# Key selection with three bits per two chunks and a third block on ScalarE; differential attention with its first odd scores in banks 4 to 7

## The reference

```
def diff_attention(q, k, v, lam, rel_bias):      # 4 heads, 8 query blocks of 128
    sc = einsum('cbhqd,cbhkd->cbhqk', qblk, kt) + bias      # c = 0, 1
    p = softmax(sc, axis=-1)
    a = p[0] - lam * p[1]
    return einsum('bhqk,bhkv->bhqv', a, vt)

def sparse_attention(q, k, v, q_idx, k_idx, w_idx):
    ...
    score = einsum('bth,bths->bts', wb, relu(logits))
    score = where(causal, score, -inf)
    _, idx = top_k(score, 256)
    ...                      # softmax attention over the 256 keys of each query
```

## Time and profile before

| what | us |
| --- | --- |
| median of 3 runs | 3103.51 |
| lowest and highest | 3095.89, 3104.91 |
| the profiled execution | 3112.71 |
| its span | 3110.2 |
| TensorE busy | 2694.9 |
| VectorE busy | 2020.7 |
| ScalarE busy | 1566.0 |
| GpSimd busy | 1153.8 |

### The profile page before, as it was taken

How to read it: one execution, slowest core, us unless ns; L and a number is a source line. 1 busy time by engine, 2 the same in 40 slices (tenths; PEclk the granted TensorE clock), 3 DMA queues, 4 the chain that set the end, 5 groups by cost and what they waited for, 6 DMA issues and landing times. The chain is left out here.

```text
span 3110.2 us, 41522 instructions
## 1 busy us (share of the span) xinstructions
PE 2694.9 (87%) x14032; PEld 2113.8 (68%) x14032; DVE 2020.7 (65%) x4318; ACT 1566.0 (50%) x3035; POOL 1153.8 (37%) x981
## 2 busy tenths in 40 slices
PE   6999788898979997988989796997889696997887
PEld 5877565676868775656777585775667584775666
DVE  4472377798434724877984348897767348897766
ACT  3221276798322113767872216675764316675761
POOL 0100166665001002765640002983741002983731
PEclk9999898999989997999999899998999899998899
DMA  4443210100324421101013110110031101110022
GB/s 123 119 139 102 85 40 8 41 1 33 117 70 124 143 82 37 39 8 41 1 56 128 51 24 24 48 45 24 1 120 71 61 21 28 48 41 25 1 88 81
DMA packets 90750, 181.93 MB, mean 58 GB/s; under 512 B 12552, under 2 KB 27912, under 8 KB 90504
## 3 DMA queue, kind: packets, MB, share of 16 engines
q1 hardware_dynamic: 74124, 150.69, 15.4%
q10 hardware_dynamic: 16416, 28.61, 3.2%
HBM read 149.87 MB, written 33.33 MB: 59 GB/s over the span
## 5 line engine op out<-in xcount | busy, mean ns | idle before, releaser
L1355 POOL TENSOR_SCALAR a_prob<-a_prob,a_ratio 128x1024 f32<-128x1024 f32 x64 | 71.9, 1123 | 536.7 <-DVE a_ratio L1314 536.7
L718 PE MATMUL ps<-w_hi,hh 128*128 128x512 f32 (+1 forms) x640 | 242.7, 379 | 22.2 <-DVE w_lo L603 10.1
L718 PE MATMUL ps<-w_lo,hh 128*128 128x512 f32 (+1 forms) x640 | 241.0, 377 | 0.0
L718 PE MATMUL ps<-w_hi,hl 128*128 128x512 f32 (+1 forms) x640 | 239.3, 374 | 0.0
L1792 PE MATMUL ps<-o_w_hi,hh 128*128 128x512 f32 x512 | 212.1, 414 | 24.3 <-DVE o_w_lo L1716 24.3
L2253 DVE TENSOR_SCALAR_CACHE_REDUCE select_rows<-masks,select_cuts 128x1024 bf16<-128x1024 int16 (+7 forms) x264 | 231.2, 879 | 0.2
L1792 PE MATMUL ps<-o_w_hi,hl 128*128 128x512 f32 x512 | 207.6, 406 | 0.0
L1792 PE MATMUL ps<-o_w_lo,hh 128*128 128x512 f32 x512 | 206.7, 404 | 0.0
L1303 DVE CUSTOM_DVE_ANT_0 a_prob<-ps,a_bias 128x1024 f32<-128x1024 f32 x128 | 151.6, 1222 | 83.2 <-PE ps L1443 83.2
L1772 POOL TENSOR_TENSOR o_rstd<-o_rstd,nhalf 128x1 f32<-128x1 f32 x56 | 46.6, 833 | 411.9 <-DVE o_rstd L1653 238.7
L1034 POOL TENSOR_SCALAR b_prob<-b_prob,a_guest_small 128x1024 f32<-128x1024 f32 x128 | 144.2, 1127 | 129.4 <-DVE a_guest_small L978 126.8
(11 more groups left out here) (356 smaller groups left out, 7942.5 us busy)
## 6 DMA issues: line engine op xcount, KB each, us to landing
w_early<-in_w_in SPq DMA_DIRECT2D x108, 256.0 KB, 2.8
ada_w<-in_w_ada ACTq DMA_DIRECT2D x96, 256.0 KB, 2.8
w_raw<-in_w_in SPq DMA_DIRECT2D x84, 256.0 KB, 2.8
ak<-gates SPq DMA_DIRECT2D x32, 256.0 KB, 3.8
xcur<-aq SPq DMA_DIRECT2D x16, 512.0 KB, 3.8
y<-xcur SPq DMA_DIRECT2D x16, 512.0 KB, 3.7
a_bias<-bias_tiles SPq DMA_DIRECT2D x8, 960.0 KB, 5.2
bq<-in_w_out SPq DMA_DIRECT2D x12, 512.0 KB, 4.1
```

The source lines that it names most:

```text
L718: mm = nc.tensor.matmul(o, lhs, rhs, start=(k == 0 and i == 0), stop=(k == K - 1 and i == 2))
```

## The change

In differential attention scores 1, 3 and 5 go to banks 4 to 7 (`score_bank`), VectorE's shift reads them there (`scores_of`), scores g up to 6 wait for the shift of g - 2 in place of g - 1, and the first transpose of probabilities waits for the shifts of steps 0 to 5. From step 7 on everything is as before.

In key selection ScalarE also counts the 384-key block (block 2) in the first 8 bits: a third Sign pass, verdict and move for each of these bits, with a third column in four small tiles. VectorE orders that block's bits before it gives ScalarE its start, goes over three blocks in the first 8 bits, then waits for ScalarE's eighth bit, takes over the negated cut and goes on with four. ScalarE's bits stand elsewhere in its list: two in each of chunks 3, 5, 7, 9 and 11, one in 4, 6, 8, 10, 12 and 13; for the second half two in chunks 17, 21 and 25 and one in each of the others from 18 to 29.

```diff
+def score_bank(g):
+    return 4 if g < 6 and g % 2 else 0
+
+def scores_of(g, m):
+    b = score_bank(g) + 2 * m
+    return ps[:, b:b + 2, :].rearrange("p b n -> p (b n)")
...
-    out=row, in0=ps[:, 2 * m:2 * m + 2, :].rearrange("p b n -> p (b n)"), in1=bias, scale=-1.0,
+    out=row, in0=scores_of(g, m), in1=bias, scale=-1.0,
...
 def turn(e):
...
+    if e == ("attn", 0, 0):
+        pe.wait_ge(shifted, 12)
...
 def scores(g):
...
-    if g >= 1:
-        pe.wait_ge(shifted, 2 * g)
+    if g >= 2:
+        pe.wait_ge(shifted, 2 * g if g > 6 else 2 * (g - 1))
...
-                mm = nc.tensor.matmul(ps[:, 2 * m + e, :], nat[rows, 0, q, q_cols],
+                mm = nc.tensor.matmul(ps[:, score_bank(g) + 2 * m + e, :], nat[rows, 0, q, q_cols],
...
-BY_DVE, BY_ACT = [7, 3, 4, 2], [5, 6]
+BY_DVE, BY_ACT, LENT = [7, 3, 4, 2], [5, 6], 8
...
+def settled_by(bits):
+    return 2 * bits + min(bits, LENT)
...
 def find_bit(i):
...
-    for j, qb in enumerate(BY_ACT):
+    blocks = BY_ACT + BY_DVE[3:] if i < LENT else BY_ACT
+    for j, qb in enumerate(blocks):
         if i >= 1:
-            act.wait_ge(moved, 2 * (i - 1) + j + 1)
+            act.wait_ge(moved, settled_by(i - 1) + j + 1)
+        if j == 2:
+            act.wait_ge(counted, settled_by(i) + 1)
         n = (qb + 1) * P
-        nc.scalar.activation(spare[:, 2 + j, 0:n], scores(qb) if half else upper(qb), ACT.Sign,
+        nc.scalar.activation(spare[:, 2 + j % 2, 0:n], scores(qb) if half else upper(qb), ACT.Sign,
...
-    for j in range(2):
-        act.wait_ge(counted, 2 * i + j + 1)
+    for j in range(len(blocks)):
+        act.wait_ge(counted, settled_by(i) + j + 1)
...
-    while found < 2 * BITS and found < (ch if ch <= BITS else BITS + 1.25 * (ch - BITS - 2)):
+    while found < 2 * BITS and found < (min(BITS, 1.5 * (ch - 2)) if ch < BITS else
+                                        BITS + 1.25 * (ch - BITS)):
...
 for half in range(2):
...
+    if not half:
+        last = mark(order_bits(BY_DVE[3]))
     after(last)
     nc.vector.memset(negcut[:, :], 0.5 - HALF_RANGE / 2 if half else 0.5).then_inc(keys_ready, 1)
-    for qb in BY_DVE:
+    for qb in BY_DVE if half else BY_DVE[:3]:
...
     for bit in range(BITS - 1, -1, -1):
-        for i, qb in enumerate(BY_DVE):
+        counted_here = BY_DVE[:3] if not half and bit >= BITS - LENT else BY_DVE
+        if not half and bit == BITS - LENT - 1:
+            weigh(BY_DVE[2], bit + 1)
+            move(BY_DVE[1], bit + 1)
+            move(BY_DVE[2], bit + 1)
+            dve.wait_ge(moved, settled_by(LENT))
+            settled[BY_DVE[3]] = mark(nc.vector.tensor_scalar(column(cut, BY_DVE[3]), negcut[:, 2:3], -1.0,
+                                                              None, ALU.mult))
+            open_ends = False
+        else:
+            open_ends = bit < BITS - 1
+        for i, qb in enumerate(counted_here):
...
-            if i >= 1 or bit < BITS - 1:
-                weigh(BY_DVE[i - 1], bit if i >= 1 else bit + 1)
-            if i >= 2 or bit < BITS - 1:
-                move(BY_DVE[i - 2], bit if i >= 2 else bit + 1)
+            if i >= 1 or open_ends:
+                weigh(counted_here[i - 1], bit if i >= 1 else bit + 1)
+            if i >= 2 or open_ends:
+                move(counted_here[i - 2], bit if i >= 2 else bit + 1)
```

More of the change, by code:

```diff
@@ L2113, in select_project_phase @@
         kept = sb("select_kept", [P, 4])
-        negcut = sb("select_negcuts", [P, 2])
-        signs = sb("select_signs", [P, 2])
-        verdict = sb("select_verdicts", [P, 2])
-        middle = sb("select_middles", [P, 2])
+        negcut = sb("select_negcuts", [P, 3])
+        signs = sb("select_signs", [P, 3])
+        verdict = sb("select_verdicts", [P, 3])
+        middle = sb("select_middles", [P, 3])
         raw = early.ring(w_raw, R)
@@ L2189, in find_bit @@
                         act.wait_ge(keys_ready, half + 1)
[L2190 removed]
+                    blocks = BY_ACT + BY_DVE[3:] if i < LENT else BY_ACT
+                    for j, qb in enumerate(blocks):
                         if i >= 1:
[L2192 removed]
+                            act.wait_ge(moved, settled_by(i - 1) + j + 1)
+                        if j == 2:
+                            act.wait_ge(counted, settled_by(i) + 1)
                         n = (qb + 1) * P
[L2194 removed]
+                        nc.scalar.activation(spare[:, 2 + j % 2, 0:n], scores(qb) if half else upper(qb), ACT.Sign,
                                              bias=negcut[:, j:j + 1], accum_out=signs[:, j:j + 1]).then_inc(counted, 1)
[L2196 to L2197 removed]
+                    for j in range(len(blocks)):
+                        act.wait_ge(counted, settled_by(i) + j + 1)
                         nc.scalar.activation(verdict[:, j:j + 1], signs[:, j:j + 1], ACT.Sign,
                                              bias=middle[:, j:j + 1]).then_inc(judged, 1)
[L2200 to L2201 removed]
+                    for j in range(len(blocks)):
+                        act.wait_ge(judged, settled_by(i) + j + 1)
                         nc.scalar.activation(negcut[:, j:j + 1], verdict[:, j:j + 1], ACT.Identity,
@@ L2220, in _ @@
                 for j, qb in enumerate(BY_ACT):
-                    act.wait_ge(moved, 2 * (2 * BITS - 1) + j + 1)
+                    act.wait_ge(moved, settled_by(2 * BITS - 1) + j + 1)
                     nc.scalar.activation(verdict[:, j:j + 1], negcut[:, j:j + 1], ACT.Identity,
@@ L2225, in _ @@
                     n = (qb + 1) * P
-                    act.wait_ge(judged, 2 * 2 * BITS + j + 1)
+                    act.wait_ge(judged, settled_by(2 * BITS) + j + 1)
                     nc.scalar.activation(spare[:, 2 + j, 0:n], scores(qb), ACT.Sign, bias=verdict[:, j:j + 1],
@@ L2285, in weigh_gate @@
                                                    ALU.mult).then_inc(weighed, 1)
-                for j, qb in enumerate(BY_ACT):
+                for j, qb in enumerate(BY_ACT + BY_DVE[3:]):
                     mark(nc.vector.memset(middle[:, j:j + 1], float((qb + 1) * P - 2 * TOPK + 1)))
@@ L2328, in _ @@
                         negative = negcut[:, j:j + 1]
-                        dve.wait_ge(moved, 4 * BITS)
+                        dve.wait_ge(moved, settled_by(2 * BITS))
                         dve.wait_ge(above, j + 1)
```

4 lines of the change are left out of this document (1 added, 3 removed).

## The result

The changed kernel took 3087.23 us (median of 6 runs, 3075.94 to 3094.07) against 3104.21 us of the kernel before beside it on the chip (6 runs, 3095.89 to 3108.78): ratio 0.9947, 95% interval 0.9923 to 0.9972, which is 17 us saved (9 to 24). Its profiled execution took 3083.4 us.

The account below looks back on a forecast made before the run. Bounds: a start-up chain with no busy engine in differential attention, VectorE in key selection. 19.0 + 4.2 = 23.2 us off the profiled 3112.7 gives 3089.5, or 3080.3 against the median 3103.5; own range 3074 to 3087, full 3072 to 3095.

Parts of the forecast that it names:

- first rival: Differential attention: start-up gain partly paid back by late GpSimd combines, 8 to 12 us kept; 3087 to 3092; chance 0.15.
- second rival: Key selection gives nothing or a little loss, ScalarE late at all three read-outs; 3084 to 3089; chance 0.09.
- Start of differential attention, 19.0 us: First transposes 20.1 us after the first shift; 9.0 and 10.9 us gained, 0.9 taken off, carried through; bounds 10 to 22.3.
- ScalarE's bit with three blocks, 3.64 us: Key selection: with the 384-key block added, one ScalarE bit takes 3.64 us, against 2.68 for two blocks.
- The read-outs late by 1.6 us a layer: Key selection: ScalarE reads out banks late by 0.5, 0.3 and 0.8 us, moving TensorE's end about 1.6 us a layer.
- The bound of 5: Key selection: TensorE's end up to 5 us late if each read-out is late by a whole chunk's excess, 2.2 us.
- VectorE ahead by 10.6 us at its masks: Key selection: the 8.2 us wait gone plus 2.9 less 0.5 from the third block puts VectorE 10.6 us ahead.
- low end of 2.9: Key selection: dropping the 384-key count in eight bits saves VectorE 2.9 to 5.8 us; 2.9 was taken.
- The end of selection, -4.2 us: Key selection ends 2.1 us sooner a layer, 4.2 in all, between 8.4 gained and -2.
- second one: Key selection, second condition: gate products wait for TensorE's last banks; end at 2135.8 against 2138.46, a gain of 2.7 us.
- The first one: Key selection, first condition: the 1024-key mask waits for GpSimd's last gate, put at 2111.1; end of masks at 2134.3.
- bound (2.6 us): Key selection: GpSimd's last gate up to 2.6 us later from running beside masks; end 2136.9, a gain of 1.6.

Follow-up runs that it names:

- With the read-outs in time: Changed kernel with none of ScalarE's bits in chunks 9, 17 and 25, right ahead of its bank read-outs: 3083.01 us, ratio 0.9921 to the kernel before.
- ranks in place alone: Changed kernel with each mask's rank scanned in place, so masks don't wait for GpSimd's last gate: 3078.43 us, ratio 0.9907 to the kernel before.
- the fastest kernel: Changed kernel with mask ranks scanned in place, no ScalarE bits right ahead of read-outs, gate products after the fourth mask: 3072.58 us, ratio 0.9888 to the kernel before.

## Why the prediction was right, and where its terms were off

The forecast was 3080.3 (3072 to 3095), faster; measured 3087.2, faster. Against the same medians it said 23.2 us and the time gave 17. The number lies at the edge of the forecast's own range (3074 to 3087), at the edge of the first rival's (3087 to 3092) and inside the second rival's (selection gives nothing, 3084 to 3089), and that second rival is what happened. The full range took in all three, so the number alone says little for the sum: its large term was right, its small one was not.

- *Start of differential attention, 19.0 us.* Right in mechanism and size: lengths of 382.3 (mean of four, kernels with the old banks) and 372.4 (four of the changed kernel and of the bank change alone) make 9.9 a layer, 19.9 in all, and the bank change alone was timed at 19. Step by step, from the first shift's start: shift 1 ended at 4.66 us (forecast 5.23), since scores 0 and 1 took 4.79 us together and not twice 2.93; the first combine came at 5.15 (forecast 5.80); four combines took 3.56 us each, and then one thing was missed: the value split in VectorE's list between shift 2 and the second ratio. It held GpSimd 1.57 us, so the transposes came at 21.15 and not at 20.1. At the transposes the gain was thus 7.9 and 9.9 us, 17.8 and not 19.9. Scores 7 did run slower than before (2.40 and 2.61 us against 1.65), 1.7 us in sum where 0.9 was taken off. That the stages gave 9.6 and 12.1 us all the same was not in the sum: 1.1 of it came between shifts 7 and 8 of layer 0, the rest I have not traced, so that the total fits as well as it does is in part luck.
- *The start-up gain is partly paid back* (the first rival, 0.15): false, the lead of layer 0 is 9.0 us at shift 8 and 9.5 at shift 28.
- *ScalarE's bit with three blocks, 3.64 us*: 3.67. The read-outs late by 1.6 us a layer in sum: TensorE's three waits grew by 0.59 + 0.28 + 0.81 = 1.7 in layer 0 and by 0.28 + 0.30 + 0.81 = 1.4 in layer 1. Right. What I did not have is what a late read-out does to the matmuls behind it: two chunks partly at the low level cost 1.5 us each, so that TensorE ended 4.9 us late in layer 0 (1.5 in layer 1, where it didn't happen). The bound of 5 in the forecast was for another reason.
- *VectorE ahead by 10.6 us at its masks*: 14.2 (158.2 us after the order-bits pass, 172.4 before). The three-block bits saved 4.5 us by the run without them, more than the low end of 2.9 that I took.
- *The end of selection, -4.2 us.* This is the step that failed. The two stages gave +1.3 and -2.0 us, -0.7 in all, and +1.2 and +1.8 with the selection changed alone. The term that was mis-sized is TensorE's lateness, 1.6 us a layer in the sum. Where the clock stayed up (layer 1) TensorE was 1.5 us late, and the stage gained the 2 us that the forecast had for a layer. Where it fell behind two read-outs (layer 0, and both layers of the selection alone) TensorE was 4.9 us late, and the stage got longer. With the read-outs in time the layers gained 2.8 and 2.9 us, more than was forecast.
- *Which condition ends the stage.* I let the second one do it (the gate products wait for TensorE), with the gates 1.6 us late. The first one did: in ten of the twelve stages with that wait (six kernels, two layers) the last mask ends 23.6 us after the last gate (181.6 + 23.6 = 205.2; 178.5 + 23.6 = 202.1; 177.6 + 23.6 = 201.2), in the other two 24.3. The last gate came 6.6 and 3.4 us later than before in the changed kernel, with TensorE 4.9 and 1.5 us late, and 2.5 us later with the read-outs in time, from running beside two masks. That contention was in the text as a bound (2.6 us) and as the Trainium skill's rule, by which the first condition ends the stage, as it did. The choice cost little: by the second condition (TensorE's end, 0.7 and 12.6) the masks would have ended at 204.6 and 201.3 us, not 205.2 and 202.1.

## What to carry to other kernels

Before work is taken off an engine, look for the next thing that it waits for at that place; ScalarE's third block bought VectorE 4.5 us here that it then stood waiting, and it shortened the stage (by 2.0 us a layer) only once the masks no longer shared a tile with the gates. The gain at a start-up chain can be carried whole through a stage whose steps are chained to one another. When an engine's list is reordered, check what TensorE does in the new gap: a wait of 2 to 4 us was in some stages paid twice, once as a wait and once in the matmuls behind it, and in others not.

## What the runs showed of the chip

- A wait of TensorE in the middle of steady work can be paid twice. In the changed kernel the granted clock fell to 1.2 GHz in chunks 8 and 24 of layer 0, after waits of 1.95 and 2.17 us, and stayed at 2.4 GHz in chunk 24 of layer 1 after the same 2.17 us, and in the three chunks after waits of 1.64 to 1.66 us; with all six waits at 1.36 it never fell. The fall came about 1.1 and 1.3 us after work had begun again (1962.7 and 2058.3), not in the wait. "TensorE: Matmul & The Clock Gate" (Part 1) of the Trainium skill has the clock low by default and released by sustained activity; the return to 2.4 GHz within the same chunk agrees with that.
- The length of the wait alone does not decide it. Over all kernels chunk 8 had slow matmuls (7.2 us where 5.67 is usual) in the six stages with 1.86 to 1.95 us ahead of it and in none with 1.77 or less. But chunk 24, after 2.17 us in twelve stages, was slow in seven and not in five. With ranks in place alone the last chunk took 5.5 us after 2.88 us in layer 0 and 7.0 after 2.43 us in layer 1. The mixing took 9.5 to 9.6 us after 3.92 and 4.01 us, and its usual 7.21 after 2.04 and 2.15 us.
- VectorE's counts (1.28 us for 1024 keys, 1.27 without GpSimd) are as long beside GpSimd as without it; in the changed kernel 55 of them lie beside its passes (nine tenths of each or more) and two clear of them. The masks are not: their scan of 1024 took 3.26 us beside GpSimd and 2.29 without, the last pass of 1024 1.67 and 0.75. GpSimd's own passes beside the first two masks of the changed kernel stretched in six of eight cases, from 1.30 to between 1.48 and 2.21.
- A shorter selection was at times followed by a longer second attention (202.1 and 136.9, 205.2 and 133.2, 200.6 and 137.1 us), and the long ones had the lower clock shown above. First order-bits pass to the end of that attention is 346.2 and 346.6 us before, 345.6 and 346.1 changed, 342.2 and 342.7 in the fastest kernel: stages that meet at a seam have to be measured together.
